# A decoder trunk in split fp32 matmuls: the start addresses of its SBUF tensors

## What is computed

```python
x = x + chunked_sgu_mixer(x, ...)          # gelu(rms(x) @ w_in) -> u, v; u * (W_s ln(v) + b); @ w_out
x = x + swiglu_ffn(x, layer 0)             # (silu(h @ w_gate) * (h @ w_up)) @ w_down, h = rms(x)
k, v = shared_kv(x)                        # rms(x) @ w_k with a norm per head, rms(x) @ w_v
x = x + moba_attention(x, k, v)            # one block of 256: causal softmax attention, @ w_o
x = x + swiglu_ffn(x, layer 1)
```

## Time and profile before

| | |
|---|---|
| runs | 2182.95, 2183.17, 2183.39 us, median 2183.17 |
| span of the profiled execution | 2180.6 us |
| PE busy | 2157.6 us (99%) |
| weight loads busy | 1775.2 us (81%) |
| DVE, ACT, POOL busy | 1118.2, 998.3, 29.6 us |
| mean granted clock | 0.998 |
| DMA | 402.47 MB, 185 GB/s |

### The profile page before, as it was taken

The page is one execution under the profiler, slowest core; times in us unless marked ns, Lnnn a source line. Parts: engine busy times, 40 slices in busy tenths (PEclk is TensorE's granted clock), DMA queues, the critical chain, the costliest instruction groups (busy, mean ns, idle before and its releaser), DMA issues.

```text
span 2180.6 us, 25371 instructions
## 1 busy us (share of the span) xinstructions
PE 2157.6 (99%) x9745; PEld 1775.2 (81%) x9745; DVE 1118.2 (51%) x1222; ACT 998.3 (46%) x1229; POOL 29.6 (1%) x37
## 2 busy tenths in 40 slices
PE   7999999999999999999999999999999999999999
PEld 6888888888888888888888888788888888888887
DVE  4566554455445444444556566554554455444443
ACT  5444454444444444434566565554444444443332
POOL 0000000000000000000000000000000000000000
PEclk9999999999999999999999999999999999999999
DMA  8655555556555555554654444456655555555553
GB/s 290 193 172 176 175 184 188 189 191 192 189 186 187 189 191 188 179 193 138 229 187 162 172 169 144 152 191 192 192 191 179 189 191 192 190 182 187 193 188 121
DMA packets 202057, 402.47 MB, mean 185 GB/s; under 512 B 6576, under 2 KB 6672, under 8 KB 201744
## 3 DMA queue, kind: packets, MB, share of 16 engines
q1 hardware_dynamic: 200896, 398.53, 55.4%
q10 hardware_dynamic: 1104, 3.15, 0.4%
HBM read 399.56 MB, written 2.10 MB: 184 GB/s over the span
## 4 chain that ended last, share of the span: by engine, by line
PE 98%; issue 0%; DMA 0%; DVE 0%; ACT 0%; SPq 0%; POOL 0%; ACTq 0%; DVEq 0%
PE acc L914 31%; PE acc L918 31%; PE acc L916 31%; PE tr L941 2%; DMA res<-in_x_dram 0%; PE tr L985 0%; PE tr L1059 0%; PE tr L1049 0%; PE tr L1067 0%; PE acc L941 0%; PE tr L1077 0%; PE tr L1076 0%; PE tr L1058 0%; PE tr L1075 0%; ACT w_hi L352 0%
## 5 line engine op out<-in xcount | busy, mean ns | idle before, releaser
L643 DVE TENSOR_TENSOR w_lo<-raw,w_hi 128x1024 fp32r<-128x1024 f32 x656 | 801.8, 1226 | 890.6 <-ACT w_hi L352 890.4
L352 ACT ACTIVATE w_hi<-raw 128x1024 fp32r<-128x1024 f32 x656 | 692.5, 1059 | 954.7 <-PE acc L918 954.7
L914 PE MATMUL acc<-w_hi,a_hi 128*128 128x512 f32 x2048 | 806.3, 394 | 4.3 <-DVE w_lo L643 4.3
L918 PE MATMUL acc<-w_hi,a_lo 128*128 128x512 f32 x2048 | 798.8, 390 | 0.0
L916 PE MATMUL acc<-w_lo,a_hi 128*128 128x512 f32 x2048 | 798.2, 390 | 0.0
L914 PEld LDWEIGHTS acc<-w_hi,a_hi 128*128 128x128 f32 x2048 | 385.5, 188 | 83.3 <-issue 4.7
L918 PEld LDWEIGHTS acc<-w_hi,a_lo 128*128 128x128 f32 x2048 | 385.1, 188 | 81.0
L916 PEld LDWEIGHTS acc<-w_lo,a_hi 128*128 128x128 f32 x2048 | 385.5, 188 | 78.5
L914 PE MATMUL acc<-w_hi,h_hi 128*128 128x512 f32 x704 | 277.9, 395 | 0.0
L918 PE MATMUL acc<-w_hi,h_lo 128*128 128x512 f32 x704 | 277.4, 394 | 0.0
L916 PE MATMUL acc<-w_lo,h_hi 128*128 128x512 f32 x704 | 277.4, 394 | 0.0
(11 more groups left out here) (110 smaller groups left out, 775.6 us busy)
## 6 DMA issues: line engine op xcount, KB each, us to landing
raw<-in_ffn_w_gate_dram SPq DMA_DIRECT2D x88, 1024.0 KB, 5.2
raw<-in_ffn_w_up_dram SPq DMA_DIRECT2D x88, 1024.0 KB, 5.2
raw<-in_ffn_w_down_dram SPq DMA_DIRECT2D x88, 1024.0 KB, 5.0
raw<-in_a_w_in_dram SPq DMA_DIRECT2D x32, 1024.0 KB, 5.4
raw<-in_a_w_out_dram SPq DMA_DIRECT2D x16, 1024.0 KB, 5.0
raw<-in_w_v_dram SPq DMA_DIRECT2D x16, 1024.0 KB, 5.0
raw<-in_w_k_dram SPq DMA_DIRECT2D x16, 1024.0 KB, 5.0
raw<-in_b_w_q_dram SPq DMA_DIRECT2D x16, 1024.0 KB, 5.0
```

The costliest lines, as they stand in the source:

```text
L352: nc.scalar.activation(dst, src, ACT.Copy).then_inc(hi_split, 1)
L643: nc.vector.tensor_tensor(lo, src, hi, ALU.subtract).then_inc(lo_split, 1)
L914: nc.tensor.matmul(acc[s][t][:, :], hi[:, kb, tok], w_hi[:, slot, k, :], start=kb == 0, stop=False)
L918: ins = nc.tensor.matmul(acc[s][t][:, :], lo[:, kb, tok], w_hi[:, slot, k, :], start=False, stop=kb == HG * n - 1)
```

## The change

Two tensors are allocated that nothing reads or writes. The first, ahead of `raw`, is 96 floats (384 bytes) a partition and moves the first group of tensors to a multiple of 512 bytes. The second, behind `row_inv`, is 112 floats (448 bytes) and does the same for the scopes behind it. No instruction changes.

```diff
+LINE = 512
+FIRST = 16512
+SMALL = 1088
...
+        sb("edge_low", [P, (-FIRST % LINE) // 4], F32)
         raw = sb("raw", [P, RAW, 2 * HG, CH], F32)
         w_hi = sb("w_hi", [P, RING, HG, CH], F32R)
...
         row_inv = sb("row_inv", [P, TT], F32)
+        sb("edge_high", [P, (-SMALL % LINE) // 4], F32)
```

## The result

The changed kernel takes 2164.15 us (median of four, 2164.10 to 2164.26) against 2183.06 us for the kernel before: a ratio of 0.9912, with a 95% interval of 0.9900 to 0.9924. It is faster by 18.9 us, which is small but well outside the scatter. The forecast was 2065 us in a range from 2050 to 2168; the time is that of the first rival, 2165 us.

What follows compares the result with a forecast made beforehand. PE, busy 99% of the span, bounds the kernel: 9024 matmuls times their start-to-start spacing. Gains of 69.1 + 51.0 - 2 = 118 us took 2183.2 to 2065 us, range 2050 to 2168.

Steps and rivals of the forecast that it cites:

- rival 1: All matmuls: only distance between the two streams counts; `a` stays, others reach 226.9 ns; 18.4 us gained, 2165 us; chance 0.30.
- two paces: Matmul spacing before: 226.9 ns with `a_hi`/`a_lo` stationary (remainder 128), 233.3 ns with `g`, `h`, `o` (remainder 192).
- Two points at 32 and 48 cycles: Excess over 512 cycles a matmul, for stationary tensors at remainder 128 and 192 bytes, 32 and 48 fp32 elements.
- 69.1 us for the `a` matmuls: Gain claimed for 6144 matmuls going from 226.9 to 215.6 ns, less 0.3 us for the slow first stretch.
- 51.0 us for `g`, `h` and `o`: Gain claimed for 2880 matmuls with these stationary tensors, going from 233.3 to 215.6 ns.
- a fixed 2.3 ns a matmul: Small fixed piece read from transposes (109 ns against 106.7), added to 213.3 ns for the columns.
- 2.6 us: Time around the profiled span: span 2180.6 against the runs' median 2183.17 us; assumed to stay.
- the lower bound, 2050 us: Bottom of the forecast range, said to stand for about 214.5 ns a matmul; 213.3 ns would give 2042 us.
- 215.6 ns: Spacing forecast for every 512-column matmul at remainder 0: 213.3 ns for the columns plus 2.3 ns.
- the feeding holds at that pace: ACT, DVE and DMA keep PE supplied when a half group of 12 takes 2.59 us instead of 2.72.
- the 2 us of slack: Loss allowed where hooks crowd ACT and DVE, about the size of the one `o_lo` wait; subtracted from the gain.

Runs made afterwards that it cites:

- All at 64: Two 448-byte pads added to the kernel before, so moving and stationary tensors all begin at remainder 64 of 512 bytes (distance 0); 2166.28 us.
- distances 128 and 192: Kernel before plus a 128-byte pad between weights and activations: `a` tiles 128 bytes, `g`, `h`, `o` 192 from the moving tiles' start, modulo 512; 2203.49 us.
- The bf16 kernel: Kernel before with all split operands in bf16 instead of fp32r, same allocation pattern; 2068.57 us (median of four), ratio 0.9474.
- at 80: Kernel before with moving tiles shifted by 240 bytes: `g`, `h`, `o` at distance 80, `a` at 16 modulo 256; 2232.78 us.
- distances 256 and 320: Kernel before plus a 256-byte pad between weights and activations: `a` tiles at distance 256, `g`, `h`, `o` at 320; 2183.96 us.

## Why the prediction was wrong

**Right.** PE's pace is the whole of the time, and two paces stand in the trace by address: both held. The two known paces and their counts gave the rival's 18.4 us; the spans differ by 18.2, the medians by 18.9. Transposes, mixing, ACT, DVE and DMA moved and cost nothing.

**The step that failed** is this: "Two points at 32 and 48 cycles lie on a line through zero, excess = elements past the multiple of 512, which puts remainder 0 at no excess." Its term, 69.1 us for the `a` matmuls, measured 0, and the 51.0 us for `g`, `h` and `o` measured 18.2 to 18.9. That the measured time still lies inside the stated range is the doing of rival 1, not of this term. The two numbers matched by chance, and not even well: 226.9 ns are 32.6 cycles over 512, not 32, and the forecast took a fixed 2.3 ns a matmul besides. Less these, the excesses are 11.3 and 17.7 ns, 27 and 42 cycles, and the line through them misses zero by some 4 cycles. In the kernel before, the moving tensors had one fixed place, so the stationary tile's remainder (128 and 192) and its distance to the moving tile (0 and 64) differ by the same 64 bytes between the classes, and the trace could not choose. I had named the second reading as rival 1 and its reason, that a common shift can't matter to two streams that meet, and still gave it 0.30 against 0.44 on the strength of a match of two points by a line that I had drawn after seeing them. All at 64 (226.9 ns) is the run that refutes the line; distances 128 and 192 (232.4 and 229.0, where place alone would have given the two old paces) are the ones that bear out the distance.

**Two small slips.** What lies around the span was taken as 2.6 us, from one execution's span and the others' median; wherever both are on record for one execution they differ by 1.7 to 1.9 us. And the lower bound, 2050 us, stands for some 214.1 ns by the forecast's own sum, not 214.5.

**What was right but not for this change.** 215.6 ns as the pace without excess, and that the feeding holds at that pace. The bf16 kernel shows both: 215.8 ns, 2068.6 us against my 2065. PE's waits there:

```profile
PE acc L897 <- DVE w_lo L626: 5.7, 1, 5.7
...
PE acc L897 <- DVE o_lo L648: 2.5, 1, 2.5
...
PE tr L1050 <- ACT prob L552: 1.3, 3, 0.5
...
PE acc L897 <- DVE w_lo L630: 0.4, 2, 0.2
```

The 5.7 us at the start (4.3 before) and the 2.5 for `o_lo` were there before. New are 1.3 in three for `prob` and 0.4 in two for `w_lo`, about the 2 us of slack that I had allowed for.

**What stays open.** Why distance 0 still costs 11 ns for 4-byte operands, why the curve over the distance is jagged, and what chooses between the two rhythms at 80. Half the load didn't halve it, and shifting one of three tensors lengthened more than its own matmul. A moving tile of one type with a stationary one of the other could tell the two streams apart; it wasn't tried.

## What to carry to other kernels

For streams of fp32r matmuls like these (512 columns, a new stationary tile for each) at 2.4 GHz, put moving and stationary tiles at the same remainder of 256 bytes; which remainder it is does not matter (226.9 ns at 0, 64 and 128 alike), and being 16 bytes off cost up to 9.7 ns of 227. A trace in which one side never moves can't tell a place from a distance, so before pricing an extrapolation, look for the variable that was held fixed; a shift of everything is the cheapest test. And a law through two points found afterwards deserves less weight than a symmetry that speaks against it.

## What was not expected of the hardware

- The pace at distances 256 and 320 is that at 0 and 64, and it has one sharp best place, 226.9 ns at 0, against 231.7 and 236.6 ns only 16 bytes to either side.
- At distance 80 the same down stage runs two columns at 233.3 ns and the third at 231.2.
- With bf16 operands, 215.8 ns whatever the distance (0 and 64), and weight loads busy for 969.7 us instead of 1775.2.
- Loading half as many stationary columns (135 instead of 188 ns a load) made `a` matmuls slower, 229.6 against 226.9 ns.
- After the 2.5 us wait for the last `o_lo`, some executions run a few microseconds at the lower clock (0.84 and 0.88 in the mean of two stretches) and others don't (1.00), which is 1.6 us from one profiled execution to the next.
